# Two sparse-attention layers of a four-layer block in fp32: the compression moved ahead of the attention with its weights stationary, eight compressed heads in one job, outputs split by ACT and DVE

## What is computed

```python
def compress(k, pos, w1, b1, w2, b2):        # blocks of 32 tokens, stride 16: 15 blocks
    win = (blocks of k) + pos                # 15 rows of 32*64 = 2048 numbers
    return gelu(win @ w1 + b1) @ w2 + b2     # hidden width 256, then 64

def hybrid_mixer(h, w_in, cmp_pos, cmp_w1, ..., conv_w, w_o):
    q, kc, vc, ks, vs, kw, vw, gates, u, bg, cg = split(h @ w_in)   # 8 query heads, 2 key heads
    kc_c, vc_c = compress(kc, ...), compress(vc, ...)
    o_cmp, p_cmp = cmp_attention(q, kc_c, vc_c)    # 15 compressed keys a head
    o_sel = sel_attention(q, ks, vs, idx)          # at 256 tokens every block is selected: causal
    o_win = win_attention(q, kw, vw)               # window 512: causal
    g = sigmoid(gates)
    o_attn = g[0]*o_cmp + g[1]*o_sel + g[2]*o_win
    o_conv = bg * conv3(cg * u)
    return concat([o_attn, o_conv]) @ w_o
```

## Time and profile before

| | |
|---|---|
| median of 3 runs | 1513.74 us (1510.78 to 1513.82) |
| profiled execution | 1509.37 us |
| its span, first to last instruction | 1507.6 us |
| PE matmul busy | 1397.2 us, 93% |
| DVE busy | 994.2 us, 66% |
| ACT busy | 753.0 us, 50% |
| POOL busy | 130.9 us, 9% |
| mean granted TensorE clock | 0.964 of full speed |

### The profile page before, as it was taken

One profiled execution on the slowest core, in us unless ns is written; L12 is line 12 of the kernel. 1 busy time (PEld: TensorE's weight loads), 2 busy tenths in 40 slices (PEclk: granted clock), 3 DMA queues, 4 the chain that ended last, 5 costly groups with the idle time before them and its releaser, 6 DMA issues.

```text
span 1507.6 us, 22916 instructions
## 1 busy us (share of the span) xinstructions
PE 1397.2 (93%) x9130; PEld 1239.2 (82%) x9130; DVE 994.2 (66%) x1462; ACT 753.0 (50%) x941; POOL 130.9 (9%) x134
## 2 busy tenths in 40 slices
PE   5999998999999989879999999978699999999995
PEld 5999987789988788768999888766688788888884
DVE  5446556565765556765544464774688889898887
ACT  3445467334323235633433335651377677777672
POOL 0000022100002100031222010022100000000000
PEclk9999999999999979989999999998699999999998
DMA  6543333446533533423555544422398988988985
GB/s 224 200 169 114 146 133 112 168 142 222 190 132 126 210 133 127 168 84 140 200 192 176 191 145 167 164 90 118 122 356 318 356 336 310 372 338 320 343 335 227
DMA packets 43676, 305.87 MB, mean 203 GB/s; under 512 B 4864, under 2 KB 5120, under 8 KB 7744
## 3 DMA queue, kind: packets, MB, share of 16 engines
q1 hardware_dynamic: 41328, 295.71, 53.1%
q0 software_dynamic: 2256, 8.88, 1.7%
HBM read 303.52 MB, written 1.05 MB: 202 GB/s over the span
## 4 chain that ended last, share of the span: by engine, by line
PE 70%; DVE 11%; ACT 7%; issue 6%; DMA 4%; POOL 1%; DVEq 0%; POOLq 0%; SPq 0%; ACTq 0%
PE g_ps L541 17%; PE g_ps L543 16%; PE g_ps L542 16%; PE a_ps L541 5%; PE a_ps L543 5%; PE a_ps L542 5%; DMA raw<-w_dram 4%; ACT w_hi L1112 4%; PE a_ps L546 3%; DVE w_lo L1396 3%; PE a_ps L550 2%; PE o_ps L546 2%; ACT prob L1139 1%; DVE tiny L1443 1%; DVE x L1527 1%
## 5 line engine op out<-in xcount | busy, mean ns | idle before, releaser
L1396 DVE TENSOR_TENSOR w_lo<-raw,w_hi 128x2048 fp32r<-128x2048 f32 x240 | 548.7, 2291 | 291.9 <-ACT w_hi L1112 286.8
L1112 ACT ACTIVATE w_hi<-raw 128x2048 fp32r<-128x2048 f32 x240 | 459.0, 1913 | 235.2 <-PE a_ps L543 86.4
L541 PE MATMUL g_ps<-w_hi,x_hi 128*128 128x256 f32 (+1 forms) x720 | 247.8, 344 | 17.1 <-DVE x_lo L1493 12.7
L541 PE MATMUL g_ps<-x_hi,w_hi 128*128 128x256 f32 x880 | 254.5, 289 | 0.0
L542 PE MATMUL g_ps<-x_lo,w_hi 128*128 128x256 f32 x880 | 251.1, 285 | 0.0
L543 PE MATMUL g_ps<-x_hi,w_lo 128*128 128x256 f32 x880 | 250.9, 285 | 0.0
L543 PE MATMUL g_ps<-w_hi,x_lo 128*128 128x256 f32 (+1 forms) x720 | 241.9, 336 | 0.0
L542 PE MATMUL g_ps<-w_lo,x_hi 128*128 128x256 f32 (+1 forms) x720 | 241.5, 335 | 0.0
L541 PEld LDWEIGHTS g_ps<-x_hi,w_hi 128*128 128x128 f32 x880 | 171.3, 195 | 5.1 <-issue 5.1
L542 PEld LDWEIGHTS g_ps<-x_lo,w_hi 128*128 128x128 f32 x880 | 171.3, 195 | 0.0
L543 PEld LDWEIGHTS g_ps<-x_hi,w_lo 128*128 128x128 f32 x880 | 171.1, 194 | 0.0
(11 more groups left out here) (264 smaller groups left out, 2072.8 us busy)
## 6 DMA issues: line engine op xcount, KB each, us to landing
raw<-w_dram SPq DMA_DIRECT2D x279, 1024.0 KB, 4.9
arena<-rows_dram POOLq DMA_DIRECT2D x3, 1024.0 KB, 5.3
x<-x_dram SPq DMA_DIRECT2D x2, 512.0 KB, 7.1
extra<-extra_dram POOLq DMA_DIRECT2D x1, 1024.0 KB, 5.8
extra<-rows_dram POOLq DMA_DIRECT2D x2, 512.0 KB, 3.8
y_spare<-rows_dram POOLq DMA_DIRECT2D x4, 256.0 KB, 4.4
out_dram<-x SPq DMA_DIRECT2D x2, 512.0 KB, 2.6
extra<-gains_dram SPq DMA_DIRECT2D x1, 512.0 KB, 4.6
```

The source lines that it names most:

```text
L541: pe.matmul(ps, lh, rh, start=start, stop=False, skip_group_check=True)
L1112: act.activation(w_hi[w_place(s)][:, :], raw[PLACE[s]][:, :], ACT.Copy).then_inc(hi_done, 1)
L1396: dve.tensor_tensor(w_lo[w_place(s)][:, :], raw[PLACE[s]][:, :], w_hi[w_place(s)][:, :].bitcast(F32), ALU.subtract).then_inc(lo_done, 1)
```

## The change

- **Order of the slots.** The keys and values to be compressed come right behind slot 0 (slot 1), then queries (2, 3), keys (4), the four compression slots (5 to 8), and the convolution's six (9 to 14). The compression is done before the attention's first step.
- **Compression.** The weights are stationary, 128 columns at a time, and the block rows move: 60 columns (high and low part side by side in `xs`) against `w_hi`, 30 against `w_lo`, 128 matmuls a layer. The hidden rows come out already turned; DVE adds the two halves (`hid_sum`).
- **Gates.** The gate weights are stationary (48 columns, high and low part) and 128 tokens move: 32 matmuls; ACT copies 48 rows and two small fp32 products with a folding matrix (`fold_rows`) turn them.
- **Compressed heads.** The four jobs become one (position 2 of 9), with 16 score products, one exponential over 16 x 15 numbers and four transposes; its values are block-placed (`vcb`) and added into `o_ps` by one 128 x 256 product for each group of causal jobs.
- **Outputs.** ACT writes the high part straight from `o_ps` or `part`, DVE the low part; POOL splits nothing here. POOL clears 2048 columns at the layer's start.

The core of the diff:

```diff
-        L_STEPS = {0: (4,), 1: (5,), 2: (6,), 3: (7, 8), 4: (9, 10), 5: (11,), 6: (12,), 8: (13,), 9: (14,)}
-        STEP_ROWS, STEP_TURN, STEP_KV = 4, 5, 6
+        L_STEPS = {0: I_U, 1: I_U + 1, 2: I_C, 3: I_C + 1, 5: I_B, 7: I_B + 1}
+        STEP_KV, STEP_PARTS, STEP_OUT = 0, (6, 8), (9, 11)
...
+            def gates_part(i, l):
+                def part_of(t, ks):
+                    for k in ks:
+                        parts_come(i, t, k)
+                        to = slice(t * P, (t + 1) * P)
+                        pe.matmul(a_ps[0][0:48, to], small[:, k, 1 + l, :, :].rearrange("p a b -> p (a b)"), x_hi[:, k, to],
+                                  start=k == 0 and t == 0, stop=False, skip_group_check=True)
+                        mm = pe.matmul(a_ps[0][0:24, to], small[:, k, 1 + l, 0, :], x_lo[:, k, to],
+                                       start=False, stop=k == KD - 1, skip_group_check=True)
...
-                    w = weights(s, (KD, S))
-                    for k in range(KD):
-                        mm = parts_mm(g_ps[first % 3][0:2 * NCMP, kind * S:(kind + 1) * S],
-                                      pick((xc_hi, xc_lo), lambda t: t[:, kind, KD * h + k, :]),
-                                      pick(w, lambda t: t[:, k, :]), kind == 0 and h == 0 and k == 0,
-                                      h == 1 and k == KD - 1)
+                    wh, wl = weights(s, (KD, S))
+                    for m in range(2):
+                        at = (2 * kind + m) * 64
+                        for k in range(KD):
+                            col, row = slice(m * P, (m + 1) * P), 16 * kind + KD * h + k
+                            pe.matmul(g_ps[first % 3][:, at:at + 60], wh[:, k, col], xs[:, row, :, :],
+                                      start=kind == 0 and h == 0 and m == 0 and k == 0, stop=False, skip_group_check=True)
+                            mm = pe.matmul(g_ps[first % 3][:, at:at + 30], wl[:, k, col], xs[:, row, 0, :],
+                                           start=False, stop=h == 1 and k == KD - 1, skip_group_check=True)
...
+                    if jb["mask"] == "cmp":
+                        for t in range(NT):
+                            for p in range(NH // 2):
+                                at, g = (4 * t + p) * NCMP, p // 2
+                                for h in range(2):
+                                    rows = slice(64 * h, 64 * h + 64)
+                                    mm = mm32(a_ps[h][:, at:at + NCMP], sq[rows, p, t * P:(t + 1) * P],
+                                              kc2[rows, g * NCMP:(g + 1) * NCMP])
...
+                    if jb["blocks"] is not None:
+                        g, j = divmod(jb["blocks"], 2)
+                        mm = mm32(o_ps[:, 0:S], vcb[:, g, j, :], pcT[:, g, :], False, True)
...
-                for s in range(s0 + 1, s0 + 4):
+                for c in range(4):
+                    compress(c // 2, c % 2)
+                for s in (s0, s0 + I_Q, s0 + I_Q + 1, s0 + I_KS):
                     pe.wait_ge(g_free[s % 3], g_nth[s] + 1)
                 pe.wait_ge(gates_done, l + 1)
-                attention(pairs_sparse(l), A_L[l], lambda g: (o_free, 16 + 4 * l + g + 1) if g < 4 else
-                          (y_made, 8 + 4 * l + g - 3), between)
-                pe.wait_ge(y_split, Y_L[l] + 6)
-                out_pair(L_WO[l], OUT_L, True)
+                attention(pairs_sparse(l), A_L[l], lambda g: (s_lo, 4 * l + g + 1), between)
+                pe.wait_ge(s_lo, 4 * l + 3)
+                out_pair(L_WO[l], OUT_L, True, (s_lo, 4 * l + 4))
...
+                j = (s0 + I_W1) % 3
+                dve.wait_ge(used, s0 + I_W1 + 4)
+                ps = g_ps[j][:, 0:256].rearrange("p (a b) -> p a b", a=4)
+                chain(lambda: dve.tensor_copy(hid_sum, ps[:, :, 30:60]))
+                dve.tensor_tensor(hid_sum, ps[:, :, 0:30], hid_sum, ALU.add).then_inc(hid_added, 1)
+                ahead(s0 + I_W1 + 3)
...
                 def outputs(g):
-                    if g < 4:
-                        dve.tensor_copy(soT[:, g, :], o_ps[:, 0:S]).then_inc(o_free, 1)
+                    dve.wait_ge(s_hi, 4 * l + g + 1)
+                    dve.tensor_tensor(y_lo[:, g, :], o_ps[:, 0:S], y_hi[:, g, :].bitcast(F32), ALU.subtract).then_inc(s_lo, 1)
...
```

More of the change, by code:

```diff
@@ L132, in shape_constants @@
     c[:, C_IOTA:C_IOTA + P] = np.arange(P)
+    for part in range(2):
+        c[24 * part:24 * part + 24, C_FOLD:C_FOLD + 24] = np.eye(24)
     return c, np.stack([even, odd])
@@ L340, in pairs_even @@
                          mask="dil" if b else "causal", fox=None if b else 2 * p, gate=None, group=p,
-                         first=True, last=True, k_ready=None, v_ready=None) for p in range(HF // 2)]
+                         first=True, last=True, k_ready=None, v_ready=None, blocks=None) for p in range(HF // 2)]
         def kv_turn(l):
@@ L1131, in hi_x, with attention @@
                                    out_bank(t, b)[:, :].rearrange("p (a b) -> p a b", a=4), ACT.Copy).then_inc(n_hi, 1)
-            def attention(jobs, a0, between):
+            def attention(jobs, a0, between, group_high=None):
                 def exps(i, h):
+                    if jobs[i]["mask"] == "cmp":
+                        if h == 0:
+                            act.wait_ge(pc_ready, jobs[i]["k_ready"][1])
+                            act.activation(pc_heads, pc_heads, ACT.Exp, scale=SCALE).then_inc(ex_done, 2)
+                        return
                     n, slot = 2 * (a0 + i) + h, 2 * ((a0 + i) % AHEAD) + h
@@ L1292, in _ @@
-                attention(pairs_sparse(l), A_L[l], between)
+                for m in range(I_KS, I_W1 + 3):
+                    ahead(s0 + m)
+                act.wait_ge(hid_added, l + 1)
+                act.wait_ge(z_pad, 2 + l)
+                for kind in range(2):
+                    for m in range(2):
+                        b1 = V_B1 + 4 * l + 2 * kind + m
+                        src = hid_sum[:, 2 * kind + m, :]
+                        if kind == 0:
+                            act.activation(hid[:, 0, m, :], src, ACT.Gelu_apprx_tanh, bias=vec[:, b1:b1 + 1])
+                        else:
+                            src = src.rearrange("p (g c) -> p g c", g=2)
+                            for g in range(NKV):
+                                ins = act.activation(hid_v[:, m, g, :, 0:NCMP],
+                                                     src[:, g, :].unsqueeze(1).to_broadcast([P, 4, NCMP]),
+                                                     ACT.Gelu_apprx_tanh, bias=vec[:, b1:b1 + 1])
@@ L1293, in _, with group_high @@
+                def group_high(g):
+                    act.activation(y_hi[:, g, :], o_ps[:, 0:S], ACT.Copy).then_inc(s_hi, 1)
+                attention(pairs_sparse(l), A_L[l], between, group_high)
                 i = 3 + 2 * l
@@ L1668, in attention @@
                         group_out(jobs[i - 4]["group"])
+                for i in range(len(jobs) + 4):
+                    if not late_outputs:
+                        group_of(i)
                     if i < len(jobs):
```

367 lines of the change are left out of this document (201 added, 166 removed).

## The result

The changed kernel takes 1522.38 us, the median of 6 runs (1519.59 to 1526.24), against 1512.8 us of the kernel before (1509.84 to 1516.8): ratio 1.0063, interval 1.0046 to 1.008. It is slower by 9.6 us. Forecast were 1512 us and, most likely, a faster kernel. They are single executions. The one of the kernel before is 3.4 us faster than its median, so some 3 us of the 12.6 are spread between executions and not the change.

A forecast was written before the change was run, and what follows sets the result against it. PE was taken as the bound, with 70% of the chain, where it works or waits. Terms a to e summed to -0.9 us a layer, -1.8 for two, giving 1512 us; range 1490 to 1522.

The forecast's parts named there:

- a. gates and start: Gates and layer start: 32 products at 0.08 us replace 48, less half clock; -4.8 us, between -1.2 and -6.5.
- b. compression: Compression: 128 products, clock falling about 4 us in, 23.4 us instead of 11.4; with the tail +13.0 us.
- c. compressed heads: Compressed heads in the attention: one job instead of four, 3.8 us instead of 7.0; -3.2 us.
- d. waits: PE's waits: 2.6 us ahead of attention go; inside 11.3 instead of 12.8, two of 2.2, one of 6.4; -4.1 us.
- e. half clock in the attention: Half clock inside the attention: 3.5 us lost instead of 5.3; -1.8 us.
- behind the layer: After the sparse mixer's output slots: the prediction gave no term, so no change.
- I work out one layer and double it: Second mixer taken as built alike: -0.9 us for one layer, -1.8 for two.
- Rival 1: Clock holds through the compression: b is +2.3, a layer gains 11.6 us, 1490 us; chance 15%.
- rival 2: Compression at half clock from its start: 3.9 us a layer more than forecast, 1520 us; chance 10%.
- at nothing: Costed at zero: DVE's block sums, POOL's clearing, the gelu, one activation table load less, the weight transfers.
- Rival 3: Turned gates bring nothing: 128 moving columns cost as much as 256, clock falls; a is -1.2, 1519 us; chance 10%.
- Rival 4: Folded heads hidden behind DVE anyhow: c worth nothing, d keeps its waits; inside the forecast's upper end, no own chance.

The follow-up runs named there:

- e2: Changed kernel with each moving column of the compression repeated four times (240 and 120 instead of 60 and 30): 1508.56 us, ratio 0.9978.
- e1: Changed kernel with the compression alone back in its old form (96 products, 256 moving columns), at its new place: 1511.88 us, ratio 0.999.
- e3: Changed kernel with DVE making the low part of a group's output ahead of the row maxima of the same step: 1515.21 us, ratio 1.0019.
- e12: Changed kernel with the convolution's second half split right behind its making, the weight split behind both: 1511.42 us, ratio 1.001.
- e4: Changed kernel with the gates alone in their old form (48 products a layer, no folding): 1530.13 us, ratio 1.0101.
- e5: Changed kernel with ACT's and DVE's queues reordered: gelu and sum of the halves ahead of splits, two splits into step 0: 1536.28 us, ratio 1.0145.
- e7: e1 with ACT's and DVE's queues reordered as in e5, ACT's copy of the rows also ahead of a split: 1513.72 us, ratio 0.9992.
- e9: Changed kernel with the compressed keys and values (kc2, vcb) taken ahead of DVE's weight split in step 0: 1515.33 us, ratio 1.0029.
- e10: e8 with the edit of e9, and DVE's weight split of step 0 put off to step 1: 1479.08 us, ratio 0.9803.
- e11: e10 with the compression of e2 instead of the old form: 1480.68 us, ratio 0.9816.
- e6: e2 with ACT's and DVE's queues reordered as in e5: 1515.31 us, ratio 1.0.
- e8: e7 with the edits of e3 and e12: 1499.83 us, ratio 0.9913.

## Why the prediction was wrong, step by step

Per layer, in us, from the first product to the end of the output slots (the first five lines as in the prediction):

| | forecast | first layer | second layer |
|---|---|---|---|
| a. gates and start | -4.8 | -5.2 | -3.6 |
| b. compression | +13.0 | +13.8 | +13.9 |
| c. compressed heads | -3.2 | -2.6 | -2.6 |
| d. waits | -4.1 | -3.0 | -3.5 |
| e. half clock in the attention | -1.8 | -0.4 | +1.4 |
| not assigned | | +0.3 | +0.2 |
| sum | -0.9 | +2.9 | +5.8 |
| behind the layer | 0 | +2.6 | +3.7 |

Term c is priced at the full clock in both kernels. Term e is half of the time in which PE works at the half clock behind the compression; half clock in a wait costs nothing. For the first layer of the kernel before these stretches are

```profile
615.00:618.40 3.40, 3.40 (x17) 0.50 0.93 364
659.40:669.60 10.20, 7.20 (x22) 0.50 0.31 104
676.50:679.90 3.40, 3.40 (x10) 0.51 0.18 27
```

and of the changed kernel

```profile
612.60:616.00 3.40, 3.40 (x18) 0.50 0.29 123
643.30:646.70 3.40, 3.40 (x20) 0.50 0.00 0
660.30:663.70 3.40, 3.40 (x15) 0.51 0.00 0
667.20:670.60 3.40, 3.04 (x7) 0.50 0.58 243
```

That is 7.0 us lost before and 6.6 now; in the second layer 6.7 and 8.1.

a. Right in mechanism. The price of the new form was 0.06 us, not 0.08: it was the low end of the bounds, half of a 256-column product. In the second layer the kernel before kept the full clock between the two halves of its gates (24 products of slot 0 in 3.2 us, 4.5 in the first), so only 3.6 came. The step that fails is "I work out one layer and double it".

b. Right, to 0.8 us: the clock fell 3.9 us in, where "about 4 us in" was forecast. What was short is the tail: first scores and slot lost 1.9 us together, not 1.5, and the run itself 23.6 to 23.9. Rival 1 (the clock holds) and rival 2 (half clock from the start) did not happen. The Trainium skill's page "TensorE: Matmul & The Clock Gate", in its table "Why this matters for your kernels", asks for no gaps between bursts. The trace has no gap ahead of the fall, and e2 removed the fall by moving columns alone, so here that rule is not enough. The section "LDWEIGHTS (loading the stationary operand)" of the same page of the Trainium skill gives the stationary columns divided by 1.2 GHz, an estimate of 107 ns for 128: the trace agrees at the full clock (0.11 us) and shows 0.21 at half, as before.

c. The total is 0.6 us too favourable, and that near only by luck, since two errors cancel in part: the 16 score products cost 1.9 us and not 1.1, since the "x8" in a row of before is the count of 8 records of 4 products; the block products cost 0.3 us and not 0.53. The keys and values for the block form cost 0.4 more.

d. Sized too favourably by about 1 us. The two waits of 2.2 us came out at 2.25. The third was 3.9 and not 6.4. DVE's 8.4 us were right (659.1 to 667.5 us), but PE had 4.6 us to do beside them and not 2.0: a wait of 0.8 us, and its products at half clock. In e1 and e2, where they run at full clock, the wait is 5.4 us. Missed were the 1.7 us for kc2, which stayed as before, and two of the three of 0.7 to 0.8 us. 12.4 us stand against 11.3. e3 and e12 show that the three large ones are no property of the output's new way: they are the order of DVE's queue.

e. The term that was mis-sized most inside the layer: -1.8 was forecast, -0.4 and +1.4 came, 4.6 us short in the two. The kernel before lost 7.0 us and not 5.3, since half clock already stood ahead of 665.5 us. But where 3.5 us were expected to be left, at the first output slot and one or two other places, the clock was down in four stretches in each layer, 6.6 and 8.1 us.

Behind the layer. The prediction gave what follows the mixer no term, that is nothing, and no reason for it; 6.3 us stand there. 2.6 are the start of the feed-forward layer, where the wait ahead is 3.1 us in both kernels and the clock was full only in the kernel before. 1.1 are half clock ahead of the experts. 2.6 are waits of PE in the experts, 4.6 us where it was 2.0, mostly for split weights.

The terms of both layers and the time behind them were forecast at -1.8 us and stand at +15.0, 16.8 us more (the 2.2 us ahead of the layers go the other way). The missing term behind the layer is 6.3 of these and term e 4.6; a to d together are 5.4, and 0.5 is not assigned. What part of the 6.3 is the change is open. The first 36 products of the feed-forward layer take 7.0 to 7.1 us in the changed kernel and in e4, e5, e7, e9, e10 and e11, 5.6 to 5.9 in e1, e2, e3, e6, e8 and e12, and 4.4 only in the one trace of the kernel before. PE waits 2.5 us in the experts of e4 and 5.3 in those of e12, where the code is the same. Why the clock is down there was not settled.

The cost "at nothing" of the gelu and the weight transfers held, but only because the compression was slow. e1 and e2 show what it hid: ACT's and DVE's queues were 4 to 6 us behind a fast one. For a clock that holds, the prediction had the next slot "already split"; in e2 it was not (DVE's split waited 3.4 us for ACT's high part), and that is one reason why rival 1's 1490 us is too low. The prediction should have said what this cover hides, as it said of the others.

Rival 3 did not happen (0.06 us a product). Rival 4 (the folded heads were hidden behind DVE anyhow) was not tested; the sum of c and d speaks against it.

## What to carry to other kernels

A product with few moving columns cost its stationary load here (0.11 us), and in a run of 128 of them most cost twice that, because the clock fell; repeating the moving columns in the access pattern cured it, worth 9 us in 24. It shortened the whole kernel only as far as the queues behind it could follow. When a stage becomes faster, look at once at what stands in each engine's queue between it and the next use: three small edits of DVE's order (keys ahead of a weight split, a low part ahead of the maxima, a split behind its maker) were worth 5, 7 and 8 us, and one edit made without reading the queue cost 12 us. e10, which has these three, the reordered queues and the old form of the compression, is 30 us faster than the kernel before, where the change alone is 10 us slower. Never double one layer's account without looking at the second.

## What was not expected of the hardware

Four times the moving columns made the same work 9.2 us faster (23.6 to 14.4 us for 128 products), though PE streams 180 columns on average instead of 45. In a pair of them the price is split by columns, 0.17 us for 240 and 0.055 for 120, and the pair costs what two loads do, 0.22. A product of 48 or 24 stationary and 128 moving columns costs 0.06 us, half of what a 128-column load costs.
